# Feeding a short causal convolution: lagged rows copied between partitions instead of loaded back from memory

## The chip, the cores and the metric

One core of one Trainium2 chip. The metric is the device time of one execution in microseconds; where a kernel was run several times, the median is given. One more execution was recorded by the hardware profiler, and every duration and time of day below (us from the start of its span) is from that one.

## The reference

One step of a hybrid decoder layer for a prompt of 512 tokens, 16 meta tokens ahead of it, and 8 decode sequences of 8 tokens, all in float32. One projection of the normed tokens gives, among others, 1536 columns for the gated-DeltaNet heads (512 each for q, k and v). These go through a causal convolution of width 4 over the tokens:

```python
xpad = jnp.concatenate([conv_prev, qkv_pre], axis=1)
conv = sum(conv_w[j] * xpad[:, j:j + t] for j in range(CONV_W))
conv = jax.nn.silu(conv)
```

For the prompt `conv_prev` is zeros, for the decode sequences it is a stored state of three rows. So output row r needs the projected rows r-3, r-2, r-1 and r. q and k are then scaled to unit length per head, and the recurrence, a differential attention (paged past keys and values for the decode sequences), an output projection, and a mixture of experts follow: per token 8 heads of 16 experts out of 16384, whose two rows of 1024 are gathered.

## The kernel before

Tokens lie on partitions: four prompt tiles of 128 rows, and one tile of 80 (64 decode tokens and the 16 meta tokens), which is called the sample tile here and always comes first. The projection is cut into units, one for a section of 512 columns and a tile: 16 matmul records of PE into one of two PSUM banks. The three convolution sections come first, so there are 15 convolution tiles, numbered m = 0 to 14; m = 0, 5 and 10 are the sample tile, the other 12 are prompt tiles.

The way of one prompt tile m through the engines:

- ACT copies the unit's bank to SBUF, scaled (`unit_copy`, L1027), into `raw[:, m % 2]`, and issues the store of these 128 rows to a buffer `pre_conv` in DRAM (L1031).
- POOL waits for the stores of tiles m and m-1 and for the SiLU of tile m-2, whose buffer it reuses, and issues one load of 128 x 4 x 512 (`conv_inputs`, L935): partition r gets the rows r-3 to r, so every row of `pre_conv` is read four times. For a sample tile there are five loads (L932, L933), and ahead of them the reload of the tap weights `cw` for the section (L918), which waits for the multiply of the tile before.
- DVE multiplies the 2048 columns by the tap weights (L1444), adds them in pairs (L1446, L1447); ACT takes the SiLU (L1128) and sums squares per head (L1138); DVE adds eps (L1454), POOL takes the power -1/2 (L886), DVE scales (L1459, L1461); SP stores the tile to DRAM (L696).

In the same stretch PE works through the decode sequences' attention over the past, in four passes p = 0 to 3 (`past`: scores L2074, folding L2090, values L2102), each with DVE sums (L1638, L1639) ahead of an exponential on ACT (L1252), three small DVE steps (L1646 to L1648) and PSUM copies on ACT (L1257, L1258). The gate columns (L1829) and the first steps of the recurrence (L1901 after L1503) lie between.

The order of the instructions on every engine is fixed when the kernel is built: each helper is a generator that yields a due time and then emits its instructions, and each engine's list is made by running the generator with the smallest due time next. `conv_at(m)` is the due time of the multiply of tile m; the units' ends give it.

The stages of a run: up to some 508 us projection, convolution, past attention, the recurrence of the first tiles and the choice of experts for the first prompt tile; from there to the end POOL gathers expert rows (8 KB each for 128 tokens, L977), DVE multiplies them with the tokens (L1797) and PE adds them up (L2228), with the attention and recurrence of the later tiles in between.

Of the kernel before, what the change touches and what calls it, by code (L numbers as in the profile page):

```python
# [27 lines left out]
HW = NH * HD  # L28
# [55 lines left out]
KEPT = (6, 2)  # L84
DMA_RING = 2048


# [163 lines left out]
def hybrid_step(nc: bass.Bass, i, o, stay_table, early_table, past_table):  # L251

    ctx = ExitStack()
    with ctx:
# [234 lines left out]
        def pre_rows(t):  # L489

            if t < PT:
                r = PRE_PROMPT + META + 128 * t
                return [(0, 128, pre[r:r + 128, :])]
            return [(0, NSAMP, samp_rows[:, CONV_W - 1:, :]), (MROW, META, pre[PRE_PROMPT:PRE_PROMPT + META, :])]

        def raw_count(n):

            return sum(2 if m % NT == 0 and m < 3 * NT else 1 for m in range(n % 2, n + 1, 2))

        def conv_loads(m):  # L500

            return sum((1 if k % NT else 1 + CONV_W) for k in range(m + 1) if conv_buffer[k] == conv_buffer[m])

# [3 lines left out]

        def taps(first, rows, ch):

            return bass.AP(tensor=pre.tensor, offset=pre.offset + first * CONV + ch.start, ap=[[CONV, rows], [CONV, CONV_W], [1, HW]])  # L510

# [145 lines left out]
        with nc.Block() as block:  # L657
# [198 lines left out]
            def _(pool):  # L856
# [52 lines left out]
                def conv_inputs():  # L909
                    for m in range(3 * NT):  # L910
                        sec, n = divmod(m, NT)
                        t = ORDER[n]
                        ch = slice(sec * HW, (sec + 1) * HW)
                        yield conv_at(m) - 9
                        if n == 0:
                            if m:
                                pool.wait_ge(s_conv, 3 * (m - 1) + 1)
                            pool.dma_start(cw, i["conv_w"][0:1, :, ch].broadcast_to([128, CONV_W, HW])).then_inc(s_cw, 16)  # L918
                        yield conv_at(m) - 8
                        if conv_before(m):  # L920
                            pool.wait_ge(s_cs, conv_before(m))
                        else:
                            pool.wait_ge(s_ss, (1, 3)[m])
                        pool.wait_ge(s_raw[m % 2], 16 * raw_count(m))
                        if n:
                            pool.wait_ge(s_raw[(m - 1) % 2], 16 * raw_count(m - 1))
                        else:
                            pool.wait_ge(s_vecs, 112)
                        b = conv_buffer[m]
                        if t == PT:  # L930
                            for j in range(CONV_W):
                                pool.dma_start(cv[b][0:NSAMP, j, :], samp_rows[:, j:j + DS, ch]).then_inc(s_cv[b], 16)  # L932
                            pool.dma_start(cv[b][MROW:LAST, :, :], taps(0, META, ch)).then_inc(s_cv[b], 16)  # L933
                        else:
                            pool.dma_start(cv[b][:, :, :], taps(META + 128 * t, 128, ch)).then_inc(s_cv[b], 16)  # L935

# [43 lines left out]
            def _(act):  # L980
# [29 lines left out]
                def unit_copy(n):  # L1010
# [9 lines left out]
                    if g < 4:  # L1020
                        c = n - C0
                        if c >= 2:
                            act.wait_ge(s_raw[c % 2], 16 * raw_count(c - 2))
                        else:
                            act.wait_ge(s_ss8, c + 1)
# [92 lines left out]
                def conv_silu(m):  # L1118
# [3 lines left out]
                    yield conv_at(m) + 4.5  # L1122
                    act.wait_ge(s_conv, 3 * (m + 1))
                    if m == 1:
# [245 lines left out]
            def _(dve):  # L1370
# [66 lines left out]
                def conv(m):  # L1437
# [5 lines left out]
                    dve.wait_ge(s_cw, 16 * (sec + 1))  # L1443
                    count.done(nc.vector.tensor_tensor(x, x, cw[0:rows], ALU.mult), s_conv)  # L1444
                    yield conv_at(m) + 2.5
# [834 lines left out]
```

## Time and profile before

| | us |
|---|---|
| median of three runs | 2042.04 (2041.55 to 2044.48) |
| the profiled execution's own time | 2041.71 |
| its span | 2039.9 |
| PE busy | 1684.6 (83%) |
| DVE busy | 1350.9 (66%) |
| ACT busy | 795.9 (39%) |
| POOL busy | 770.7 (38%) |

How to read it: the span runs from the first to the last recorded event of the core. A busy share is an average over all stages, and each stage has its own limit; so the stages have to be looked at by themselves. Instructions of an engine run in program order, and idle time of an engine stands ahead of the instruction that waited, with what released it. Idle time matters only where it is handed on to the engine that paces the stage.

### The profile page before, as it was taken

How to read it: one execution, taken by the hardware profiler on the slowest of the kernel's cores; microseconds unless marked ns; L12 is line 12 of the kernel's file. 1: busy time of each engine (PE TensorE's matmuls, PEld its weight loads, DVE VectorE, ACT ScalarE, POOL GpSimd, SP SyncE). 2: the span in 40 equal slices, each digit the busy share in tenths (PEclk: the TensorE clock that was granted, in tenths of full speed). 3: DMA queues.
4: the chain of work that ended last, by engine and by line, in shares of the span. 5: the costliest groups of instructions: out<-in, count | busy, mean ns of one | idle time of the engine just before them, and what ended most of it. 6: DMA issues, size and time to landing. Idle time of an engine off the chain costs nothing.

```text
span 2039.9 us, 20195 instructions
## 1 busy us (share of the span) xinstructions
PE 1684.6 (83%) x6163; PEld 849.3 (42%) x6163; DVE 1350.9 (66%) x3035; ACT 795.9 (39%) x2359; POOL 770.7 (38%) x670
## 2 busy tenths in 40 slices
PE   7898899988998878889787888977897657866877
PEld 2334364547453344445334444533463223532211
DVE  1344514345898666887766788775698977679544
ACT  1334312222546433563543346362344433333432
POOL 2211100111444433435454353633444555554442
PEclk9998899999999988999999899998999788987999
DMA  9999623138999999999999999999999999999997
GB/s 345 369 370 369 215 79 114 47 119 330 395 423 413 428 427 428 426 420 410 427 415 429 426 426 403 420 425 394 425 427 427 427 427 427 427 427 427 427 428 314
DMA packets 137301, 759.68 MB, mean 372 GB/s; under 512 B 15295, under 2 KB 24399, under 8 KB 60760
## 3 DMA queue, kind: packets, MB, share of 16 engines
q0 software_dynamic: 88448, 622.22, 73.5%
q1 hardware_dynamic: 44112, 124.93, 16.4%
q10 hardware_dynamic: 4632, 11.23, 1.4%
q8 instruction: 49, 0.80, 0.1%
q14 instruction: 60, 0.49, 0.1%
HBM read 742.35 MB, written 16.26 MB: 372 GB/s over the span
## 4 chain that ended last, share of the span: by engine, by line
PE 34%; DMA 34%; DVE 17%; ACT 7%; issue 5%; POOL 3%; SPq 0%; ACTq 0%; DVEq 0%; POOLq 0%
DMA sb_uv<-in_peer_uv,sb_eidx 29%; PE bank L2228 14%; DVE sb_uv L1797 7%; PE bank L1818 7%; PE bank L2195 3%; DVE sb_hres L1770 2%; POOL sb_uv L977 2%; DMA sb_hres<-pre_conv 2%; ACT sb_diag L1367 1%; PE bank L2137 1%; DMA sb_w<-in_w_sections 1%; DMA sb_zone<-in_w_route 1%; PE bank L1932 1%; ACT sb_ew L1360 1%; PE bank L1944 1%
## 5 line engine op out<-in xcount | busy, mean ns | idle before, releaser
L2228 PE MATMUL bank<-sb_uv,sb_diag 128*128 128x512 f32 (+1 forms) x1812 | 926.3, 647 | 274.8 <-ACT sb_diag L1367 265.0
L977 POOL DMA_INDIRECT sb_uv<-in_peer_uv,sb_eidx x576 | 689.3, 1197 | 845.7 <-PE bank L2228 647.7
L1797 DVE CUSTOM_DVE_ANT_0 sb_uv<-sb_uv,sb_xn 128x1024 f32<-128x1024 f32 x576 | 699.6, 1220 | 295.5 <-DMA sb_uv<-in_peer_uv,sb_eidx 292.9
L2228 PEld LDWEIGHTS bank<-sb_uv,sb_diag 128*128 128x128 f32 (+1 forms) x1812 | 325.5, 195 | 756.2 <-ACT sb_diag L1367 441.8
L1356 ACT ACTIVATE sb_gel<-sb_h 128x1 f32<-128x1 f32 x576 | 116.2, 202 | 769.4 <-DVE sb_h L1797 767.0
L1818 PE MATMUL bank<-sb_w,sb_xnT 128*128 128x512 f32 (+1 forms) x560 | 267.3, 619 | 16.8 <-DVE sb_xnT L1385 8.3
L1367 ACT ACTIVATE sb_diag<-sb_stay,sb_ew 128x128 f32<-128x128 f32 (+1 forms) x453 | 178.4, 394 | 45.3 <-PE bank L2228 3.4
L1360 ACT ACTIVATE sb_ew<-sb_gel,sb_gate 128x1 f32<-128x1 f32 x576 | 169.7, 295 | 20.1 <-ACT sb_gel L1356 0.4
L1770 DVE SCALAR_TENSOR_TENSOR sb_hres<-sb_uv,sb_ew,sb_hres 128x1024 f32<-128x1024 f32 x123 | 157.5, 1281 | 4.1 <-ACT sb_ew L1360 4.1
L1818 PEld LDWEIGHTS bank<-sb_w,sb_xnT 128*128 128x128 f32 (+1 forms) x560 | 98.3, 187 | 139.7 <-issue 118.3
L2195 PEld LDWEIGHTS bank<-sb_rT,sb_zone 128*128 128x128 f32 x1024 | 124.1, 195 | 20.9 <-issue 20.1
L2195 PE MATMUL bank<-sb_rT,sb_zone 128*128 128x128 f32 x1024 | 125.6, 279 | 2.5 <-issue 1.8
L901 POOL TENSOR_TENSOR sb_rstd<-sb_ms,sb_minus_half 128x8 f32<-128x8 f32 (+1 forms) x10 | 16.4, 1642 | 113.2 <-DVE sb_ms L1472 113.2
L1797 DVE DVE_READ_ACCUMULATOR2_ANT sb_h<- 128x1 f32 x576 | 46.9, 81 | 0.0
L1356 ACT ACT_TABLE_LOAD x33 | 42.3, 1283 | 0.6
L1444 DVE TENSOR_TENSOR sb_xin<-sb_xin,sb_taps 128x2048 f32<-128x2048 f32 (+1 forms) x8 | 18.3, 2288 | 33.9 <-DMA sb_xin<-pre_conv 33.9
L1701 DVE FIND_INDEX8 sb_tix<-sb_top,sb_score 128x8 uint32<-128x128 f32 x144 | 38.4, 283 | 0.0
L1444 DVE TENSOR_TENSOR sb_hres<-sb_hres,sb_taps 128x2048 f32<-128x2048 f32 (+1 forms) x7 | 16.0, 2292 | 30.2 <-DMA sb_hres<-pre_conv 30.2
L1697 DVE MAX8 sb_top<-sb_score 128x8 f32<-128x128 f32 x144 | 31.4, 278 | 7.0 <-ACT sb_score L1328 6.9
L2137 PE MATMUL bank<-sb_mix_kept,sb_rT 128*128 128x512 f32 x64 | 31.3, 626 | 4.4 <-ACT sb_rT L1283 3.6
L1536 DVE TENSOR_TENSOR sb_X<-sb_X,bank 128x256 f32<-128x256 f32 (+1 forms) x36 | 14.7, 407 | 30.4 <-PE bank L1944 28.8
L2195 PEld LDWEIGHTS bank<-sb_rT,sb_held 128*128 128x128 f32 x256 | 31.9, 197 | 6.8 <-issue 6.8
(352 smaller groups left out, 1610.9 us busy)
## 6 DMA issues: line engine op xcount, KB each, us to landing
sb_zone<-in_w_route SPq DMA_DIRECT2D x14, 2304.0 KB, 12.2
sb_w<-in_w_sections SPq DMA_DIRECT2D x40, 512.0 KB, 8.9
sb_uv<-in_peer_uv,sb_eidx POOLq DMA_INDIRECT x576, 14.0
sb_sS<-in_cache_kT SPq DMA_DIRECT2D x32, 256.0 KB, 8.4
sb_zone<-in_cache_kT SPq DMA_DIRECT2D x32, 256.0 KB, 7.3
sb_held<-in_cache_v SPq DMA_DIRECT2D x32, 256.0 KB, 9.2
sb_zone<-in_cache_v SPq DMA_DIRECT2D x32, 256.0 KB, 9.5
sb_hres<-pre_conv POOLq DMA_DIRECT2D x6, 1024.0 KB, 8.9
```

The source lines that it names most:

```text
L977: nc.gpsimd.indirect_dma_start(uv[:, m % RING, :], None, i["peer_uv"], bass.IndirectOffsetOnAxis(ap=eidx[:, t % 2, n:n + 1], axis=0)).then ...
L1356: nc.scalar.activation(G["gel"][:, at], G["h"][:, at], ACT.Gelu).then_inc(s_dg, 1)
L1360: nc.scalar.activation(G["ew"][:, at], G["gel"][:, at], ACT.Copy, scale=gate[:, t % 2, n:n + 1]).then_inc(s_dg, 1)
L1367: nc.scalar.activation(G["diag"][:, d % DIAGS, 0:cols], eye, ACT.Copy, scale=G["ew"][:, at]).then_inc(s_dg, 1)
L1444: count.done(nc.vector.tensor_tensor(x, x, cw[0:rows], ALU.mult), s_conv)
L1701: n_used = count.inc(nc.vector.max_index(tix[:, q, k:k + 8], top[:, q, k:k + 8], sets[q]), s_cut if k and q == quads[-1] else s_tk)
L1770: nc.vector.scalar_tensor_tensor(hres[:, t % 2, :], uv[:, m % RING, D:2 * D], G["ew"][:, m % 8:m % 8 + 1], hres[:, t % 2, :], ALU.mult, AL ...
L1797: nc.vector.tensor_tensor_reduce(out=uv[:, m % RING, 0:D], in0=uv[:, m % RING, 0:D], in1=xn2[:, t % 2, :], scale=1.0, scalar=0.0, op0=ALU. ...
L1818: ins = nc.tensor.matmul(bank[b][0:rows, :], lhsT=xT(t)[:, kk, :], rhs=F["w"][:, piece % PIECES, kk % 2, :], start=kk == 0, stop=kk == KC - 1)
L2137: ins = nc.tensor.matmul(bank[6 + half][:, :], lhsT=R["rT"][:, k, :], rhs=mixer_row(n, half, k), start=k == 0, stop=k == KC - 1)
L2195: ins = nc.tensor.matmul(bank[6 + j % 2][:, 128 * s:128 * s + 128], lhsT=weights_part(n, g + 2)[:, k, 128 * s:128 * s + 128], rhs=R["rT"][ ...
L2228: ins = nc.tensor.matmul(bank[half][0:rows, :], lhsT=G["diag"][:, d % DIAGS, 0:rows], rhs=uv[:, m % RING, D + 512 * half:D + 512 * half + ...
```

## The change

For the 12 prompt tiles the taps no longer come from DRAM. Three copies within SBUF, issued by POOL, take rows j to j+124 of `raw` to partitions 3 to 127 of tap j (j = 0, 1, 2). Tap 3, which has no lag, is not copied: DVE multiplies it straight out of `raw`. Only what crosses a tile's edge goes through DRAM: ACT stores the first and the last three rows of a tile (two stores of 3 rows instead of one of 128), and POOL loads 3 rows x 3 taps for partitions 0 to 2. So a prompt tile has four POOL-issued transfers instead of one, and the multiply is two instructions. Counts of the semaphores follow. The reuse of `raw` by ACT now also waits for the multiply of the tile that used it before. The sample tiles are unchanged.

```diff
+EDGE = CONV_W - 1
...
             if t < PT:
                 r = PRE_PROMPT + META + 128 * t
-                return [(0, 128, pre[r:r + 128, :])]
+                return [(first, EDGE, pre[r + first:r + first + EDGE, :]) for first in (0, 128 - EDGE)]
...
         def raw_count(n):
-            return sum(2 if m % NT == 0 and m < 3 * NT else 1 for m in range(n % 2, n + 1, 2))
+            return sum(2 if m < 3 * NT else 1 for m in range(n % 2, n + 1, 2))
+        def conv_steps(m):
+            return sum(4 if k % NT else 3 for k in range(m))
         def conv_loads(m):
-            return sum((1 if k % NT else 1 + CONV_W) for k in range(m + 1) if conv_buffer[k] == conv_buffer[m])
+            return sum((CONV_W if k % NT else 1 + CONV_W) for k in range(m + 1) if conv_buffer[k] == conv_buffer[m])
...
-        def taps(first, rows, ch):
-            return bass.AP(tensor=pre.tensor, offset=pre.offset + first * CONV + ch.start, ap=[[CONV, rows], [CONV, CONV_W], [1, HW]])
+        def taps(first, rows, ch, many=CONV_W):
+            return bass.AP(tensor=pre.tensor, offset=pre.offset + first * CONV + ch.start, ap=[[CONV, rows], [CONV, many], [1, HW]])
...
                         yield conv_at(m) - 9
                         if n == 0:
                             if m:
-                                pool.wait_ge(s_conv, 3 * (m - 1) + 1)
+                                pool.wait_ge(s_conv, conv_steps(m - 1) + 2)
                             pool.dma_start(cw, i["conv_w"][0:1, :, ch].broadcast_to([128, CONV_W, HW])).then_inc(s_cw, 16)
-                        yield conv_at(m) - 8
+                        yield conv_at(m) - (12.2 if n else 8)
                         if conv_before(m):
                             pool.wait_ge(s_cs, conv_before(m))
                         else:
                             pool.wait_ge(s_ss, (1, 3)[m])
+                        if n:
+                            bank_of, copies = entry_bank("unit", C0 + m)
+                            pool.wait_ge(s_bank[bank_of], copies + 1)
+                            for j in range(EDGE):
+                                pool.dma_start(cv[conv_buffer[m]][EDGE:128, j, :], F["raw"][j:j + 128 - EDGE, m % 2, :]).then_inc(s_cv[conv_buffer[m]], 16)
+                            yield conv_at(m) - 8.6
                         pool.wait_ge(s_raw[m % 2], 16 * raw_count(m))
...
-                            pool.dma_start(cv[b][:, :, :], taps(META + 128 * t, 128, ch)).then_inc(s_cv[b], 16)
+                            pool.dma_start(cv[b][0:EDGE, 0:EDGE, :], taps(META + 128 * t, EDGE, ch, EDGE)).then_inc(s_cv[b], 16)
...
                             act.wait_ge(s_raw[c % 2], 16 * raw_count(c - 2))
+                            if (c - 2) % NT and c - 2 < 3 * NT:
+                                act.wait_ge(s_conv, conv_steps(c - 2) + 2)
...
-                    act.wait_ge(s_conv, 3 * (m + 1))
+                    act.wait_ge(s_conv, conv_steps(m + 1))
...
-                    count.done(nc.vector.tensor_tensor(x, x, cw[0:rows], ALU.mult), s_conv)
+                    if n:
+                        count.inc(nc.vector.tensor_tensor(x[:, 0:EDGE], x[:, 0:EDGE], cw[0:rows, 0:EDGE], ALU.mult), s_conv)
+                        count.done(nc.vector.tensor_tensor(x[:, EDGE], F["raw"][0:rows, m % 2, :], cw[0:rows, EDGE], ALU.mult), s_conv)
+                    else:
+                        count.done(nc.vector.tensor_tensor(x, x, cw[0:rows], ALU.mult), s_conv)
```

## Rows read from the trace of the kernel before

**Rows 1.** Busy time by stage: length; PE, PEld, DVE, ACT, POOL; clock, DMA share, GB/s.

```profile
72.00:262.00 190.00, 172.76 (x770) 76.51 (x767) 92.26 (x128) 72.46 (x195) 33.02 (x39) 0.94 0.89 321
262.00:508.00 246.00, 228.00 (x1114) 143.62 (x1112) 94.97 (x262) 57.50 (x146) 28.77 (x24) 0.99 0.38 137
508.00:2039.00 1531.00, 1233.34 (x4140) 612.12 (x4140) 1148.03 (x2620) 651.63 (x1986) 692.20 (x578) 0.93 1.00 418
```

**Rows 2.** Timeline of PE, 112 to 240 us: start, length, instruction [idle before, releaser].

```profile
112.73 1.03 PE L1829 MATMUL bank<-sb_xnT,sb_wba 128*8 128x512 f32 x4 [1.85 <-DVE sb_held L1639]
...
118.64 1.89 PE L2090 MATMUL bank<-sb_held 128*128 128x64 f32 x16
...
161.26 3.67 PE L2090 MATMUL bank<-sb_held 128*128 128x64 f32 x16 [5.38 <-DVE sb_held L1648]
...
209.52 1.07 PE L2102 MATMUL bank<-sb_held 128*32 128x512 f32 x2 [5.87 <-ACT sb_held L1258]
...
239.34 0.77 PE L1901 MATMUL bank<-sb_stay,sb_kb 80*128 80x80 f32 x4 [3.35 <-DVE sb_kb L1503]
```

**Rows 3.** The chain that ended last, around 170 us: start, length, what.

```profile
165.34 3.63 PE bank L1818 x4
...
174.37 1.87 PE bank L1818 x4
```

**Rows 4.** Timeline of DVE: multiplies of m = 3, 4, 5, 6, 9, 10 and 13.

```profile
107.07 2.29 DVE L1444 TENSOR_TENSOR sb_hres<-sb_hres,sb_taps 128x2048 f32<-128x2048 f32 x1 [4.78 <-DMA sb_hres<-pre_conv]
...
110.66 0.69 DVE L1447 TENSOR_TENSOR sb_hres<-sb_hres 128x512 f32<-128x512 f32 x1
...
123.03 2.29 DVE L1444 TENSOR_TENSOR sb_xin<-sb_xin,sb_taps 128x2048 f32<-128x2048 f32 x1 [4.70 <-DMA sb_xin<-pre_conv]
...
141.88 2.29 DVE L1444 TENSOR_TENSOR sb_hres<-sb_hres,sb_taps 80x2048 f32<-80x2048 f32 x1 [10.56 <-DMA sb_hres<-pre_conv]
...
150.13 2.28 DVE L1444 TENSOR_TENSOR sb_xin<-sb_xin,sb_taps 128x2048 f32<-128x2048 f32 x1
...
188.32 2.29 DVE L1444 TENSOR_TENSOR sb_hres<-sb_hres,sb_taps 128x2048 f32<-128x2048 f32 x1 [2.50 <-DMA sb_hres<-pre_conv]
...
203.96 2.29 DVE L1444 TENSOR_TENSOR sb_xin<-sb_xin,sb_taps 80x2048 f32<-80x2048 f32 x1 [5.16 <-DMA sb_xin<-pre_conv]
...
236.18 2.29 DVE L1444 TENSOR_TENSOR sb_hres<-sb_hres,sb_taps 128x2048 f32<-128x2048 f32 x1 [5.75 <-DMA sb_hres<-pre_conv]
```

**Rows 5.** Timeline of POOL: loads of m = 3, 4, 5 and 13, weights' reload.

```profile
95.41 0.78 POOL L935 DMA_DIRECT2D sb_hres<-pre_conv  x1 [7.29 <-issue]
...
112.08 0.79 POOL L935 DMA_DIRECT2D sb_xin<-pre_conv  x1 [10.51 <-ACT sb_cs L1128]
...
125.78 0.79 POOL L918 DMA_DIRECT2D sb_taps<-in_conv_w  x1 [10.58 <-DVE sb_xin L1444]
126.56 2.29 POOL L932 DMA_DIRECT2D sb_hres<-pre_conv  x4
...
228.94 0.80 POOL L935 DMA_DIRECT2D sb_hres<-pre_conv  x1
```

**Rows 6.** Timeline of ACT's DMA issues: stores of m = 3 and 5.

```profile
87.40 0.33 ACTq L1031 DMA_DIRECT2D pre_conv<-sb_raw  x1
...
113.92 1.11 ACTq L1031 DMA_DIRECT2D pre_conv<-sb_raw  x2
```

**Rows 7.** DMA issues of the whole span: KB each, median us from issue to landing.

```profile
sb_hres<-pre_conv POOLq DMA_DIRECT2D x6, 1024.0 KB, 8.9
...
sb_stay<-stay_tables ACTq DMA_DIRECT2D x1, 816.0 KB, 10.9
...
sb_hres<-pre_conv POOLq DMA_DIRECT2D x5, 128.0 KB, 10.7
...
sb_held<-sb_held ACTq DMA_DIRECT2D x1, 32.0 KB, 6.9
...
pre_conv<-sb_qst POOLq DMA_DIRECT2D x3, 6.0 KB, 3.2
```

## The prediction

> **What bounds the kernel now.** I read the kernel by stages first [rows 1]. The last and longest stage, 508 to 2039 us, has its DMA engines busy all the time (share 1.00, 418 GB/s): it streams expert rows, its length is given by bytes, and the change does not touch it. The stage before it, 262 to 508, has PE busy 228 of 246 us and DMA at 0.38. All the work of the change lies in the first stage, and the table's row for 72 to 262 says what to look for there: PE busy 172.8 of 190 us, at a mean clock of 0.94, beside DMA at 0.89 and DVE, ACT and POOL each under half. So PE paces that stretch, with holes, and a microsecond of hole filled there reaches the end of the run if the two later stages simply start sooner.
>
> Next the order of PE's instructions, for the holes [rows 2]: 1.85 us ahead of L1829, 5.38 ahead of L2090, 5.87 ahead of L2102, 3.35 ahead of L1901, 16.5 us in all. None is a wait for DMA; all are for DVE or ACT. Behind the second hole PE also runs at the lower of its two clock levels (1.2 instead of 2.4 GHz): the 16 matmuls of L2090 take 3.67 us where they took 1.89 at 118.64 [rows 2], and four of L1818 take 3.63 where they take 1.87 a little later [rows 3]: 3.5 us on top of the hole.
>
> Then what made DVE and ACT late. DVE runs in program order, and its long idle times stand ahead of the tap multiply L1444, waiting for loaded taps [rows 4]: 10.56 us at 141.88, 5.16 at 203.96, 5.75 at 236.18. POOL's rows [rows 5] give the other half: it issues the load of tile m=3 at 95.41 after idling 7.29 us, although ACT issued that tile's store at 87.40 [rows 6]. From store to multiply (107.07) is **19.7 us: about 8 for the store, 11.7 for the load** [rows 4 to 6].
>
> **The change, part by part.**
>
> *Bytes.* A prompt tile stored 256 KB and loaded 1024; it will move 3 x 250 KB on chip, store 12 KB and load 18: 500 KB less, 6.1 MB over 12 tiles. At 321 GB/s over a share of 0.89, so 361 at full share [rows 1], that is 17 us of DMA time. No hole of PE waits for DMA directly, so I count none of it; it can only shorten landings.
>
> *ACT.* One store becomes two. Two issues took 1.11 us from 113.92, one takes 0.33 [rows 6]: 0.78 us more per prompt tile. ACT has room for 9 us [rows 1], but the copy of m=8 stands right ahead of the exponential that the second hole waits for: 0.78 is charged there. The new wait of the copy of tile m+2 for the multiply of m costs nothing: ACT's own order has the SiLU of m, which waits for that multiply and the sums behind it, ahead of that copy. If that cover went, PE's next unit would wait for its bank.
>
> *POOL.* One issue of 0.79 us becomes four; the nearest rows, four of 64 rows in 2.29 and the 0.79 itself [rows 5], give 0.57 each, 2.3 in all: 1.5 more per tile, 18 in total, beside 33 busy of 190 [rows 1]. The order hardly moves: the copies are written as due at 12.2 before the multiply, but the stream has first to pass its step at 9 before it, so they stand where the load stood, behind the same power step of tile m-2 and ahead of that of m-1. Only tile 1's copies pass tile 0's power step. Queued behind the edge load's wait for the store is again the power of m-1, as before.
>
> *DVE.* 2048 columns in 2.29 us become 1536 and 512. Between the 512-column 0.69 and 2.29 [rows 4] a line gives 1.76 for 1536: 2.45 in all, 0.16 more per tile.
>
> *The edge's way.* Store 6 KB, wait, load 18 KB. From below, both land as the 6 KB store did early in the run, 3.2 us each [rows 7]: 7.7 us with 1.3 of issues. From above, they are as slow as now: 8 for the store, 10.7 for a 128 KB load [rows 7] and 0.6: 19.3, no gain. I take 6 us each, 13.3 in all, because the smallest transfer made under load, 32 KB, landed in 6.9 [rows 7].
>
> *The copies.* No copy of this size from SBUF to SBUF is in the trace. The 32 KB one took 6.9 us, the 1 MB load 8.9 [rows 7]. I take 9 behind 1.7 us of issues, 10.7 after ACT's copy; less than 13.3, so the edge sets the time. Ends: 6.9, and several times 9 (below). They need no store to have landed.
>
> The Trainium skill (DMA: Bandwidth & Descriptors, section "Why a DMA increments its semaphore by 16 and not by 1") speaks against the copies: a transfer is spread over the largest number of engines up to 16 that divides the slowest dimension, which is 5 for 125 rows, though it also tells of GpSimd copies on trn2 that kept 16. No row here shows a transfer of such a row count; by the first reading it is the second rival, by the other the sum stands.
>
> So a tap multiply can start some 6 us sooner after its projection, where nothing else is late. **At each hole:**
>
> A. L1829 waits for a DVE sum that stands behind m=3's multiply (107.07 [rows 4]). 6 us sooner, that hole is gone: 1.85.
>
> B. m=4's load was issued only at 112.08 [rows 5], because its store queued behind two table loads (L998, L999) on ACT's queue, the larger of which took 10.9 us [rows 7]. The edge stores queue there too, but the tables are issued behind the SiLU of m=2, which comes 4 to 6 us sooner. So the edge can be there about 114, and DVE was free at 118.33 (123.03 less 4.70) [rows 4], before A. I take m=4's multiply 6 us sooner; bounds 4.7 and 7.1. At that multiply hangs a chain that the change leaves alone: reload of the tap weights (125.78 [rows 5]), five loads of the sample tile m=5, its multiply at 141.88, m=6's directly behind it at 150.13, the exponential, L2090. All of it moves 6 us. PE resumes at 161.26 - 6 + 0.78 = 156.0: 5.2 gained, A within it. What is left of the hole is 2.8 us beside an otherwise earlier PE; I take it that the clock then stays up: 3.5. Together 8.7.
>
> C. The same chain at the third section: m=9's multiply waited 2.50 us for its load [rows 4]; that goes, then DVE's order is late next. Weights, five loads, m=10's multiply (203.96) and L2102 come 2.4 us sooner against the rest.
>
> D. m=13's load went out at 228.94, behind a power step of the decode part that stays, when DMA is light. Copies to 230.7, edge load to 231.2, landing 3.2 to 4 later, about 235 against 236.18: 1.2.
>
> Sum: 8.7 + 2.4 + 1.2 = **12.3 us**. The profiled execution took 2041.71 us, 0.33 under the median of the runs shown, which is nothing here: 2041.7 - 12.3 = 2029.4. I say **2029**.
>
> **The rivals.**
>
> *Hidden by the sample tiles.* The waits at 141.88 and 203.96 are for the loads of m=5 and m=10, which the change doesn't touch. If m=4 and m=9 gain nothing, since the edge store is held up behind the tables or small transfers under load are as slow as big ones, A and D remain: 2041.7 - 3.1 = 2038.6. For it: the upper bound of the edge. Against it: m=4 and m=9 do wait for loads on DVE.
>
> *Copies on few engines, no gain.* A 1 MB load puts 64 KB on each of 16 engines and lands in 8.9 us, 5.7 more than the 3.2 of a tiny one. If all three copies share five engines, each carries 150 KB: 3.2 + 13.4 = 16.6, and with 2.4 of copy and issues 19 us, what it is now. Then only the bytes are saved: about 2040. (If each takes another five, 50 KB each, the forecast stands.) This is what the Trainium skill's rule would do at its worst here.
>
> *Slower: one engine per copy.* Then it carries 250 KB, 22.3 + 3.2 = 25.5 us, so 28 after the projection's copy instead of 19.7. The multiply of m=4 (copy ready about 101) would come near 129 instead of 123, of m=9 near 200 instead of 188, of m=13 some 8 us late: 26 us, 2068. It decides from a landing of about 16 us on. Against it: nothing in the copies but their odd row count and their shift between partitions.
>
> *All holes close.* Lighter DMA brings the sample tiles sooner as well: 16.5 + 3.5 = 20 us, 2022, or a little below with clock losses that I left out.
>
> *The change doesn't do what it says,* for instance the copies wait for something that I took as done: 2042.
>
> **How the numbers follow.** 0.2%, 4 us, is about what a measurement of this kernel can tell from no change. Forecast 0.58, with its own range of 2021 to 2036; hidden 0.15, a third of it over 4 us faster; no gain 0.06; slower 0.10; all holes 0.08; nothing 0.03. Faster: 0.58 + 0.05 + 0.08 = 0.71; same: 0.10 + 0.06 + 0.03 = 0.19; slower 0.10. The range 2019 to 2042 takes in the forecast, the two cases without much gain, no effect and most of the closed holes: more than 8 in 10 on its face; I leave it, since the copy's landing has no row.
>
> **What the profile would show.** Right: the three copies land within 12 us of their issue; L1444 of m=4 starts by 118 and of m=5 by 137; the hole ahead of L2090 is under 3 us and its 16 matmuls take about 1.9; m=1 to 4 and 6 to 9 start some 6 us sooner after their projection; the last stage keeps its length. Wrong: copies that land after 16 us or more, POOL idle ahead of the power steps, or an equal gain at 262 that is gone at 508.

## The result, and the profile of the changed kernel

The changed kernel takes **2049.76 us** (median of 8 runs, 2045.77 to 2057.36) against 2042.25 for the kernel before beside it: ratio 1.0038, 95% interval 1.0022 to 1.0054. It is slower by 7.5 us where 13 less were forecast. Its profiled execution took 2051.02 us, with a span of 2049.2.

Busy time by stage after, columns as in [rows 1]:

```profile
72.00:262.00 190.00, 164.70 (x753) 72.15 (x752) 91.41 (x137) 70.50 (x189) 50.11 (x71) 0.93 0.90 289
262.00:508.00 246.00, 230.90 (x1126) 144.53 (x1124) 92.26 (x250) 57.31 (x147) 28.82 (x24) 0.99 0.37 133
508.00:2049.00 1541.00, 1239.69 (x4140) 614.76 (x4140) 1151.15 (x2632) 652.48 (x1988) 699.42 (x578) 0.93 1.00 416
```

In the first row PE did 8.1 us less work than before (172.76 in [rows 1]). Its last two figures are the ones to stop at: the DMA engines are as busy, 0.90 against 0.89, but move 289 GB/s instead of 321. A tenth fewer bytes take the same time.

PE's timeline after, the instructions with holes (they answer to [rows 2]; PE's line numbers are 17 higher):

```profile
109.84 3.70 PE L1835 MATMUL bank<-sb_w,sb_xnT 128*80 128x512 f32 x4 [9.61 <-DMA sb_w<-in_w_sections]
...
168.36 0.62 PE L2119 MATMUL bank<-sb_held 128*32 128x512 f32 x2 [0.82 <-DMA sb_zone<-in_cache_v]
...
185.60 9.30 PE L1835 MATMUL bank<-sb_w,sb_xnT 128*80 128x512 f32 x16 [8.89 <-DMA sb_w<-in_w_sections]
...
214.15 0.62 PE L2119 MATMUL bank<-sb_held 128*32 128x512 f32 x2 [0.71 <-ACT sb_held L1271]
...
243.16 0.77 PE L1918 MATMUL bank<-sb_stay,sb_kb 80*128 80x80 f32 x4 [5.25 <-DVE sb_kb L1520]
```

[rows 2] leave out a fifth hole of the kernel before, a short one that waits for ACT:

```profile
148.74 7.13 PE L1818 MATMUL bank<-sb_w,sb_xnT 128*128 128x512 f32 x16 [0.78 <-ACT sb_raw L1027]
```

The old holes of 1.85, 5.38 and 0.78 us are gone and 5.87 became 0.71: 13.2 us. Two new ones, 9.61 and 8.89, both wait for **the weights of the next section**; with 0.82, and 1.9 more ahead of L1918, that is 21.2. The balance is 8 us, the work that PE lacks above.

The first of these weights on SP's queue, timeline before:

```profile
91.69 1.57 SPq L687 DMA_DIRECT2D sb_w<-in_w_sections  x2
```

And in the changed kernel's chain that ended last (start, length, what):

```profile
91.73 18.07 DMA sb_w<-in_w_sections
109.84 3.70 PE bank L1835 x4
```

The issue stands at the same time in both kernels; the landing takes 18.07 us, and PE waits for its end. The second hole is another matter in part. Its weights on SP's queue, before and after:

```profile
166.93 1.86 SPq L687 DMA_DIRECT2D sb_w<-in_w_sections  x4
```

```profile
172.36 3.88 SPq L692 DMA_DIRECT2D sb_w<-in_w_sections  x4
```

They go out 5.4 us later and land in 13.7 instead of 12.1 us (medians of the four), so most of that hole comes from the late issue.

The traffic around the first moment, 78 to 112 us: packets, MB and their time as a share of 16 engines (q1 is SP's queue, q0 POOL's), then issues with KB and median us to landing. Before:

```profile
DMA packets 5614, 13.39 MB, mean 394 GB/s; under 512 B 596, under 2 KB 596, under 8 KB 5611
...
q1 hardware_dynamic: 4241, 8.47, 65.7%
q0 software_dynamic: 650, 2.47, 19.6%
...
sb_w<-in_w_sections SPq DMA_DIRECT2D x4, 512.0 KB, 11.5
```

After:

```profile
DMA packets 4872, 11.36 MB, mean 334 GB/s; under 512 B 705, under 2 KB 705, under 8 KB 4869
...
q1 hardware_dynamic: 3729, 7.32, 66.1%
q0 software_dynamic: 816, 2.34, 24.0%
...
sb_w<-in_w_sections SPq DMA_DIRECT2D x3, 512.0 KB, 18.1
...
sb_xin<-sb_raw POOLq DMA_DIRECT2D x6, 250.0 KB, 8.2
```

A share times 34 us over its MB is the **price of a megabyte** in time of all 16 engines. It is no cost in isolation: with ACT's queue the shares add up to over 100% (103 before, 104 after), so packets of different queues overlap, and a packet's time can hold some waiting. POOL's queue went from 2.70 us (0.196 x 34 / 2.47) to 3.49, and SP's queue, which does what it did, from 2.64 to 3.07. Over single packets of this stretch, the median of POOL's 4096-byte ones rose from 168 to 227 ns, the mean of SP's 2048-byte ones from 87 to 100.

The same rows for the whole front, up to the first gather of the experts, columns as above (q10 is ACT's queue). Before, 0 to 485.6:

```profile
q1 hardware_dynamic: 38592, 80.37, 46.7%
q0 software_dynamic: 5504, 18.20, 11.7%
q10 hardware_dynamic: 4632, 11.23, 6.0%
```

After, 0 to 488.6:

```profile
q1 hardware_dynamic: 38592, 80.37, 48.5%
q0 software_dynamic: 5696, 15.06, 11.3%
q10 hardware_dynamic: 3048, 8.23, 4.5%
```

Share times stretch gives 226.8 + 56.8 + 29.1 = 312.7 us before and 237.0 + 55.2 + 22.0 = 314.2 after. The stores saved 7 us; POOL's queue saved 1.6, with 17% fewer bytes; SP's unchanged traffic became 10 us dearer. **The change moves 6.1 MB less and uses no less DMA time.**

### The profile page after: what moved, and what is told of

Same layout as the page of the kernel before. It is cut to its first block, busy times and chain, and to the rows that moved or that the text cites. A ratio compares the mean times of both kernels' runs of the same rounds, so it can differ in the third digit from the quotient of the medians.

```text
span 2049.2 us, 20269 instructions
## 1 busy us (share of the span) xinstructions
PE 1687.2 (82%) x6163; PEld 849.3 (41%) x6163; DVE 1351.8 (66%) x3047; ACT 796.1 (39%) x2359; POOL 796.7 (39%) x706
## 4 chain that ended last, share of the span: by engine, by line
PE 37%; DMA 31%; DVE 14%; ACT 7%; issue 4%; SPq 4%; POOL 2%; ACTq 0%; DVEq 0%; POOLq 0%
DMA sb_uv<-in_peer_uv,sb_eidx 27%; PE bank L2245 15%; PE bank L1835 7%; DVE sb_uv L1814 6%; PE bank L2212 3%; DMA sb_w<-in_w_sections 2%; PE bank L2154 2%; POOL sb_uv L988 2%; SPq L837 1%; DVE sb_hres L1787 1%; ACT sb_diag L1380 1%; SPq L824 1%; ACT sb_ew L1373 1%; DMA sb_zone<-in_w_route 1%; SPq L819 1%
## 5 line engine op out<-in xcount | busy, mean ns | idle before, releaser
L988 POOL DMA_INDIRECT sb_uv<-in_peer_uv,sb_eidx x576 | 697.3, 1211 | 843.0 <-PE bank L2245 651.9
L2212 PE MATMUL bank<-sb_rT,sb_held 128*128 128x128 f32 x256 | 31.2, 275 | 0.0
L1949 PEld LDWEIGHTS bank<-sb_X,sb_MT 128*128 128x128 f32 (+1 forms) x184 | 23.0, 186 | 16.6 <-issue 16.6
## 6 DMA issues: line engine op xcount, KB each, us to landing
sb_zone<-in_w_route SPq DMA_DIRECT2D x14, 2304.0 KB, 12.1
sb_zone<-in_cache_v SPq DMA_DIRECT2D x32, 256.0 KB, 10.3
```

The costliest lines, as they stand in the source:

```text
L988: nc.gpsimd.indirect_dma_start(uv[:, m % RING, :], None, i["peer_uv"], bass.IndirectOffsetOnAxis(ap=eidx[:, t % 2, n:n + 1], axis=0)).then ...
L2212: ins = nc.tensor.matmul(bank[6 + j % 2][:, 128 * s:128 * s + 128], lhsT=weights_part(n, g + 2)[:, k, 128 * s:128 * s + 128], rhs=R["rT"][ ...
```

## The experiments

They ask in turn whether the copies are the cause, what makes them dear, whether their moment counts, and whether a better version follows. "Price" is that of POOL's queue in 78 to 112 us, worked out as above (before 2.70, after 3.49 us per MB). Ratios are to the kernel before, whose median was 2040.7 to 2042.2 beside these runs. The cuts of the code are shortened: `b` stands for `conv_buffer[m]`, and semaphore increments and their counts are left out. "The whole result" marks runs that leave no lag out. The expectations speak of two holes of 3.70 and 9.30 us, 13.0 in all; these are the lengths of the matmuls behind the holes. The holes are 9.61 and 8.89, 18.5 in all.

**No copies.**

```diff
-for j in range(EDGE):
-    pool.dma_start(cv[b][EDGE:128, j, :], F["raw"][j:j + 128 - EDGE, m % 2, :])
-tensor_tensor(x[:, 0:EDGE], x[:, 0:EDGE], cw[0:rows, 0:EDGE], ALU.mult)
+tensor_tensor(x[:, 0:EDGE], F["raw"][0:rows, m % 2, :].unsqueeze(1).broadcast_to([rows, EDGE, HW]), cw[0:rows, 0:EDGE], ALU.mult)
```

> The changed kernel without its 36 copies: the multiply reads the projection's buffer for all four taps (the lags of rows 3 to 127 are left out; every instruction of DVE, every store and every edge load stays). All theories of the front's transfers (copies are dear, or uneven, or shifted): the first weights of sections m = 5 and m = 10 land as early as before or earlier, the two holes ahead of L1835 (3.70 and 9.30 us) shrink to under 2 us in all, the 2.3 us holes ahead of the transposes stay away, and the mark at the first gather of the experts comes at 475 to 481 us (changed kernel 488.6, kernel before 485.6); the whole is some 8 to 12 us below the changed kernel's, so 2030 to 2036 us against the kernel before's 2042. Rival, the holes come from the new order on POOL's and ACT's queues or from the edge loads and not from copies: the holes stay near 13 us and the mark at 487 to 489. If the part of the loss behind the first gather (6 us of 9) belongs to the change and not to the run, it shows here too.

Measured: **2016.49 us**, 0.9876 (0.9856 to 0.9896): 33 us under the changed kernel, three times what was expected; the first gather comes at 459.3 instead of 488.6. The weights' matmuls as a group, 72 to 262 us (count, busy, mean ns, idle before), in the changed kernel:

```profile
L1835 PE MATMUL bank<-sb_w,sb_xnT 128*128 128x512 f32 (+1 forms) x233 | 111.7, 626 | 18.5 <-DMA sb_w<-in_w_sections 18.5
```

Without copies:

```profile
L1833 PE MATMUL bank<-sb_w,sb_xnT 128*128 128x512 f32 (+1 forms) x278 | 126.9, 600 | 0.0
```

The loss goes with the copies: ACT's split store, its wait, the edge loads and the two multiplies are all still there. DMA queues without copies up to the first gather, 0 to 459.3:

```profile
q1 hardware_dynamic: 38594, 80.40, 50.6%
q0 software_dynamic: 2816, 5.84, 4.9%
q10 hardware_dynamic: 3048, 8.23, 4.7%
```

The front's DMA time is 276.5 us, 37.7 less than in the changed kernel, and 33 of it reach the end, though no hole in [rows 2] names a DMA. That is no fixed rate: from before to after 1.5 us more came with 7.5 at the end, and the early copies of 128 rows below have 298.8 us, 13.9 less than before, for 4.9 at the end. SP's own traffic takes 232.4 us here, still 5.6 more than before: of the 10 us by which it became dearer, 4.6 go with the copies, and what the other 5.6 are no run shows.

**Source in memory; no shift.** Two runs, each with one edit to the copy:

```diff
-pool.dma_start(cv[b][EDGE:128, j, :], F["raw"][j:j + 128 - EDGE, m % 2, :])
+pool.dma_start(cv[b][EDGE:128, j, :], i["x_prompt"][0, j:j + 128 - EDGE, 0:HW])
```

> The changed kernel with only the source of the 36 copies changed: the same 125 rows of 2 KB to the same places at the same moments, after the same wait, but out of a prompt input in memory instead of the projection's buffer (so the lagged taps of rows 3 to 127 hold tokens and not the projection). Theory 1, a packet between partitions is slow in itself (median 229 ns against 169 for the 1 MB load of before) and slows the other queues: POOL's 4096-byte packets go back to 165 to 180 ns, the front's rate comes back from 334 to over 370 GB/s in the stretch 78 to 112, the holes ahead of L1835 fall from 13.0 to under 4 us, first gather at 476 to 482 us, whole 2031 to 2038. Theory 2, it is the volume and the moment of 750 KB per tile: packets and holes as in the changed kernel, first gather 487 to 490, whole 2046 to 2052.

```diff
-pool.dma_start(cv[b][EDGE:128, j, :], F["raw"][j:j + 128 - EDGE, m % 2, :])
+pool.dma_start(cv[b][EDGE:128, j, :], F["raw"][EDGE:128, m % 2, :])
```

> The changed kernel with copies of 125 rows from partition p to partition p instead of p-1, p-2 and p-3 (the lags of rows 3 to 127 are left out). Theory, the shift of partitions makes the copies dear (a packet's read and write lie at different places): packets fall from 229 ns towards 170, holes ahead of L1835 from 13.0 to under 5 us, first gather at 477 to 483 us. Theory, any copy from SBUF to SBUF is dear: nothing changes, packets 220 to 240 ns, holes 11 to 15 us, first gather 487 to 490, whole 2047 to 2052 us.

Measured: 2049.04 us, 1.0031 (1.0018 to 1.0044), price 3.39; and 2048.06, 1.0029 (1.0010 to 1.0047), price 3.53. POOL's queue with the source in memory, 78 to 112 us:

```profile
q0 software_dynamic: 816, 2.34, 23.3%
```

Neither the on-chip source nor the shift makes the copies dear. Theory 1 falls.

**Three taps from memory.** The whole result: full store, no copies, one load of 3 taps in place of 4, sent where the kernel before sends its load; last tap from the projection's buffer.

```diff
-return [(first, EDGE, pre[r + first:r + first + EDGE, :]) for first in (0, 128 - EDGE)]
+return [(0, 128, pre[r:r + 128, :])]
...
-yield conv_at(m) - (12.2 if n else 8)
+yield conv_at(m) - 8
...
-for j in range(EDGE):
-    pool.dma_start(cv[b][EDGE:128, j, :], F["raw"][j:j + 128 - EDGE, m % 2, :])
...
-pool.dma_start(cv[b][0:EDGE, 0:EDGE, :], taps(META + 128 * t, EDGE, ch, EDGE))
+pool.dma_start(cv[b][:, 0:EDGE, :], taps(META + 128 * t, 128, ch, EDGE))
```

> A version that computes the whole result: the full row block of 256 KB is stored as in the kernel before, the three lagged taps come from memory in one load of 768 KB, and only the tap without lag is read from the projection's buffer; no copy between partitions. Against the kernel before it moves 256 KB (a quarter of the load) less per prompt tile and waits for the same store. If copies are what costs: the landing of the loads shrinks from 8.9 to about 7.5 us, so L1458 starts about 1.5 us earlier than the multiply before, weights land as before (no hole over 1 us ahead of L1835), first gather 480 to 485, whole 2034 to 2041, a gain of 1 to 8 us against the kernel before. If the loss lies in the two multiplies, the waits on s_conv or ACT's added wait, which this version keeps: whole 2044 to 2050, like the changed kernel.

Measured: **2034.92 us**, 0.9969 (0.9956 to 0.9983): faster than both kernels. Its traffic in 78 to 112 us:

```profile
DMA packets 5955, 13.59 MB, mean 400 GB/s; under 512 B 661, under 2 KB 661, under 8 KB 5952
...
q1 hardware_dynamic: 4778, 9.48, 73.4%
...
q0 software_dynamic: 454, 1.66, 12.7%
```

Price 2.60. And the queues up to its first gather, 0 to 472.5:

```profile
q1 hardware_dynamic: 38594, 80.40, 48.2%
q0 software_dynamic: 4736, 15.06, 9.9%
q10 hardware_dynamic: 4632, 11.23, 6.2%
```

The front's DMA time is 303.8 us: 8.9 less than before, for 6.5 at the end. One hole for weights stays, 3.21 us at 172.87, where none over 1 us was expected.

**One copy of three taps.**

```diff
-for j in range(EDGE):
-    pool.dma_start(cv[b][EDGE:128, j, :], F["raw"][j:j + 128 - EDGE, m % 2, :])
+pool.dma_start(cv[b][EDGE:128, 0:EDGE, :], F["raw"][EDGE:128, m % 2, :].unsqueeze(1).broadcast_to([128 - EDGE, EDGE, HW]))
```

> The changed kernel with the three copies of a tile made one: one transfer writes all three taps of 125 partitions, 6 KB side by side in each, out of the same rows of the projection's buffer (from partition p to p, so the lags of rows 3 to 127 are left out, as in the run without the shift). Same bytes, same wait, same moment; 62.5 packets of 2 partitions per tap become 187.5 packets that lie in one partition. Theory A, the form (2 KB to each partition, a packet across two of them) makes a packet cost 229 ns instead of 170 and slows its neighbours: packets go to 165 to 185 ns, the two holes ahead of L1835 go from 13.0 to under 5 us, whole 2022 to 2034 us. Theory B, it is 125 rows instead of 128, or SBUF to SBUF, or the early moment: nothing changes, whole 2045 to 2052 us.

Measured: 2090.35 us, 1.0239 (1.0218 to 1.0259), price 4.44, the worst of all: the single copy lands in 10.3 to 12.3 us, and the trace has 751 packets of 8 bytes on POOL's queue in 78 to 112, where the changed kernel has 35. Where these come from is open; neither theory had them. PE does not lose its time ahead of the weights here (0.93 us) but behind DVE, whose multiplies wait for taps; the edge loads land in 15.5 and 22.6 us. In PE's timeline:

```profile
134.47 1.88 PE L1845 MATMUL bank<-sb_xnT,sb_wba 128*8 128x512 f32 x4 [18.18 <-DVE sb_held L1655]
```

**Memory in three loads.** As "three taps from memory", with:

```diff
-pool.dma_start(cv[b][:, 0:EDGE, :], taps(META + 128 * t, 128, ch, EDGE))
+for j in range(EDGE):
+    pool.dma_start(cv[b][:, j, :], taps(META + 128 * t + j, 128, ch, 1)[:, 0, :])
```

> The whole result, as in the version with three taps in one load from memory (2034.9 us), but that load of 768 KB made into three of 128 rows of 2 KB, one per tap. Theory A (form): packets go from 172 to about 225 ns, weights' landing from 11.7 to over 14 us, a hole over 5 us ahead of the weights' matmuls, whole 2043 to 2055 us: slower than the one load by 8 to 20. Theory B (125 rows, source or moment): as the one load, 2033 to 2039, only two more issues of 0.55 us on POOL per tile.

Measured: 2039.75 us, 0.9989 (0.9973 to 1.0005), price 2.65, packets 162 ns. Theory A (form) falls: 2 KB to a partition is cheap here. The 5 us against one load go with PE's holes behind DVE and ACT and not with waits for weights: 4.31, 3.57 and 4.98 us where one load has 2.44, 0.97 and 1.96.

**112 rows; copies later.**

```diff
-pool.dma_start(cv[b][EDGE:128, j, :], F["raw"][j:j + 128 - EDGE, m % 2, :])
+pool.dma_start(cv[b][16:128, j, :], F["raw"][16:128, m % 2, :])
```

> The changed kernel with three copies of 112 rows (16 times 7) from partition p to p in place of 125 rows (rows 3 to 15 of the lagged taps keep what the buffer held, the other lags are left out). 10% fewer bytes. Theory, 125 rows share out unevenly over the 16 engines: packets fall to 170 to 185 ns, weights land within 13 us, holes ahead of L1835 from 12 to 16 us (run without the shift: 12.1) to under 5, whole 2025 to 2036. Theory A (form) or early moment: packets stay over 215 ns, holes 9 to 13 us, whole 2041 to 2050 (a few us less than without the shift at 125 rows, for the bytes).

```diff
-for j in range(EDGE):
-    pool.dma_start(cv[b][EDGE:128, j, :], F["raw"][j:j + 128 - EDGE, m % 2, :])
 pool.wait_ge(s_raw[m % 2], 16 * raw_count(m))
 pool.wait_ge(s_raw[(m - 1) % 2], 16 * raw_count(m - 1))
+for j in range(EDGE):
+    pool.dma_start(cv[b][EDGE:128, j, :], F["raw"][j:j + 128 - EDGE, m % 2, :])
```

> The whole result; the changed kernel with the three copies issued behind the two waits for the stores, together with the edge load, so some 4 to 7 us later and no longer right behind the projection. Theory, the moment: copies sent earlier than the load of before collide with the section's weights; then weights of m = 5 and m = 10 land in 11 to 14 us, holes ahead of L1835 under 6 us, whole 2034 to 2043. Theory A (form): the packets stay at 220 to 235 ns and the sum of the holes at 11 to 16 us, some of them now ahead of L1658-type waits for the copies; whole 2047 to 2056.

Measured: 112 rows 2043.65 us, 1.0010 (0.9999 to 1.0020), price 3.61: no cheaper per byte although 16 divides 112. Later copies 2042.62, 1.0006 (0.9995 to 1.0018), price 3.71: as dear, yet 7 us better at the end. Its two weights' holes became one, in PE's timeline:

```profile
180.09 9.21 PE L1835 MATMUL bank<-sb_w,sb_xnT 128*80 128x512 f32 x16 [8.04 <-DMA sb_w<-in_w_sections]
```

That hole is 8.04 us where under 6 was expected, and 4.01 us for cached keys (`in_cache_kT`, at 147.28) come on top. So for dear copies the moment is worth some 7 us beside the price: sent right behind the projection they collide with the weights' landing.

**128 rows.** The cheap loads had 128 rows, the dear ones 125 or 112. Three runs; the edge load is out in each:

```diff
-pool.dma_start(cv[b][EDGE:128, j, :], F["raw"][j:j + 128 - EDGE, m % 2, :])
+pool.dma_start(cv[b][:, j, :], F["raw"][:, m % 2, :])
...
-pool.dma_start(cv[b][0:EDGE, 0:EDGE, :], taps(META + 128 * t, EDGE, ch, EDGE))
```

> The changed kernel with three copies of all 128 rows, partition p to p, out of the projection's buffer at the same early moment, and without the edge load of 18 KB that they cover (the lags of every row are left out). 2.4% more bytes than the 125 rows without the shift (packets 231 ns, 2048.1 us). Theory C, it is the rows of a transfer: with 128 rows, 8 for each of 16 engines, an engine keeps to a fixed block of partitions, with 125 or 112 the blocks lie across it; packets fall from 229 to 160 to 185 ns, the packets of the weights' queue from a mean of 98 to under 90, the holes ahead of L1835 from 12 to under 3 us, whole 2020 to 2034. Rival, copies that are sent so early are dear whatever their rows: packets 215 to 240, whole 2044 to 2052.

```diff
-pool.dma_start(cv[b][EDGE:128, j, :], F["raw"][j:j + 128 - EDGE, m % 2, :])
+pool.dma_start(cv[b][:, j, :], i["x_prompt"][0, 0:128, 0:HW])
```

> The run with the source in memory (125 rows of a prompt input, packets 227 ns, 2049.0 us) with 128 rows in place of 125, at the same early moment, without the edge load (lagged taps hold tokens). Theory C: packets 160 to 185 ns, whole 2020 to 2034 and within 5 us of the 128 rows from the projection's buffer, so that the source costs nothing. Rival, moment: 215 to 240 ns, 2044 to 2052.

```diff
-pool.dma_start(cv[b][EDGE:128, j, :], F["raw"][j:j + 128 - EDGE, m % 2, :])
+for r in (0, 64):
+    pool.dma_start(cv[b][r:r + 64, j, :], F["raw"][r:r + 64, m % 2, :])
```

> As the copies of 128 rows, but each made as two of 64 rows (partitions 0 to 63 and 64 to 127): 6 transfers per tile, 4 rows for each of 16 engines, nothing left over, but an engine's rows now lie elsewhere than in the 128-row transfers. Theory C (fixed block of partitions for each engine): packets stay dear, 200 to 240 ns, whole 2040 to 2056. Rival, a number of rows that leaves a remainder over 16 engines or an odd packet is what costs: packets 160 to 185 ns, whole 2022 to 2038, with 1.7 us more of issues on POOL per tile.

Measured: 128 rows from the projection's buffer **2035.74 us**, 0.9976 (0.9964 to 0.9988), price 2.52; early from memory 2035.83, 0.9966 (0.9950 to 0.9983), price 2.74; the same rows as two halves 2053.28, 1.0066 (1.0047 to 1.0084), price 3.80. The traffic with 128 rows, 78 to 112 us:

```profile
q1 hardware_dynamic: 4044, 8.13, 66.9%
q0 software_dynamic: 720, 2.36, 17.5%
...
sb_w<-in_w_sections SPq DMA_DIRECT2D x4, 512.0 KB, 12.4
```

The early load of 128 rows from memory:

```profile
q0 software_dynamic: 720, 2.36, 19.0%
```

And twice 64:

```profile
q0 software_dynamic: 831, 2.29, 25.6%
...
sb_w<-in_w_sections SPq DMA_DIRECT2D x3, 512.0 KB, 18.3
```

Three more rows per copy and no edge load: 12 us less than the 125 unshifted rows, and the weights land in 12.4 us (before 11.5). The edge load is not what divides them: the two halves have none either and are dear. Theory C had the side right, but both times are some 2 us above its range and one hole of 7.68 stays where under 3 was expected, in PE's timeline with 128 rows:

```profile
106.71 3.70 PE L1833 MATMUL bank<-sb_w,sb_xnT 128*80 128x512 f32 x4 [7.68 <-DMA sb_w<-in_w_sections]
```

**The kernel before again.**

> The kernel before, unchanged, for a second profile. If the 6 us that the changed kernel's profile loses behind the first gather (1560.6 us from the first gather to the end against 1554.3) are scatter of that stage, this profile takes 1556 to 1563 there and first gathers at 480 to 487; if the change slows that stage, it takes 1553 to 1556. Whole 2036 to 2047 us.

Measured: 2043.37 us. The first gathers of POOL (start) in its timeline and in the changed kernel's:

```profile
482.62 1.09 POOL L977 DMA_INDIRECT sb_uv<-in_peer_uv,sb_eidx  x1 [18.33 <-DVE sb_eidx L1754]
```

```profile
488.60 1.09 POOL L988 DMA_INDIRECT sb_uv<-in_peer_uv,sb_eidx  x1 [18.34 <-DVE sb_eidx L1771]
```

From there to the end it took 1559.0 us, against 1554.3 in the first profile and 1560.6 in the changed kernel's. So the 6 us that the changed kernel seemed to lose in the last stage are that stage's scatter (all 17 profiles lie between 1552.9 and 1563.5); against this second profile the front alone is 6.0 us later.

**Which property of 128.** Three more runs: 128 rows sent later, 120 rows from partition 8 (the whole result), 125 rows from partition 0.

```diff
-for j in range(EDGE):
-    pool.dma_start(cv[b][EDGE:128, j, :], F["raw"][j:j + 128 - EDGE, m % 2, :])
...
 pool.wait_ge(s_raw[(m - 1) % 2], 16 * raw_count(m - 1))
+for j in range(EDGE):
+    pool.dma_start(cv[b][:, j, :], F["raw"][:, m % 2, :])
...
-pool.dma_start(cv[b][0:EDGE, 0:EDGE, :], taps(META + 128 * t, EDGE, ch, EDGE))
```

> Both at once: copies of all 128 rows from p to p without the edge load (lags left out), issued behind the waits for the stores as in the run with later copies. Corners so far: 125 rows early 2048 to 2050, 125 later 2042.6, 128 early 2035.7. If rows and moment add up: 2028 to 2031 us, no hole over 2 us ahead of the weights' matmuls. If the later moment only helped because it eased the collision of dear packets: 2033 to 2038, like 128 early.

```diff
-return [(first, EDGE, pre[r + first:r + first + EDGE, :]) for first in (0, 128 - EDGE)]
+return [(first, many, pre[r + first:r + first + many, :]) for first, many in ((0, 8), (128 - EDGE, EDGE))]
...
-pool.dma_start(cv[b][EDGE:128, j, :], F["raw"][j:j + 128 - EDGE, m % 2, :])
+pool.dma_start(cv[b][8:128, j, :], F["raw"][j + 8 - EDGE:j + 128 - EDGE, m % 2, :])
...
-pool.dma_start(cv[b][0:EDGE, 0:EDGE, :], taps(META + 128 * t, EDGE, ch, EDGE))
+pool.dma_start(cv[b][0:8, 0:EDGE, :], taps(META + 128 * t, 8, ch, EDGE))
```

> The whole result: the changed kernel with the copies cut to partitions 8 to 127 (120 rows, the lag in the source), and 8 rows instead of 3 at the tile's head through memory. If a transfer is dear when an engine's run of rows straddles blocks of 8 partitions, and 120 rows fall to 15 engines in runs of 8 that begin on a block: packets 160 to 185 ns, whole 2033 to 2038, like 128 early rows. If it is dear whenever an engine writes to a block that is another engine's in the 128-row transfers (or if 120 rows are dealt out 7.5 to each of 16): 205 to 250 ns, whole 2045 to 2052.

```diff
-pool.dma_start(cv[b][EDGE:128, j, :], F["raw"][j:j + 128 - EDGE, m % 2, :])
+pool.dma_start(cv[b][0:128 - EDGE, j, :], F["raw"][0:128 - EDGE, m % 2, :])
...
-pool.dma_start(cv[b][0:EDGE, 0:EDGE, :], taps(META + 128 * t, EDGE, ch, EDGE))
+pool.dma_start(cv[b][128 - EDGE:128, 0:EDGE, :], taps(META + 128 * t, EDGE, ch, EDGE))
```

> The changed kernel with its 125 rows written to partitions 0 to 124, p to p, and the 3 edge rows written to partitions 125 to 127 (lags left out, the same bytes and transfers). If the start decides, 16 runs of 8 rows (the last of 5) that begin where those of a 128-row transfer begin: packets 160 to 185 ns, whole 2033 to 2039. If the count of 125 decides (run lengths that aren't 8): 215 to 240 ns, whole 2045 to 2052.

Measured: 128 later 2033.77 us, 0.9964 (0.9949 to 0.9979), price 2.65; 120 rows 2053.63, 1.0057 (1.0039 to 1.0074), price 3.52; 125 from partition 0 2050.54, 1.0036 (1.0023 to 1.0049), price 3.60. Later is worth some 2 us once the copies are cheap, which is within the scatter of the two: mostly it eased the collision of dear packets. Neither the start nor blocks of 8 decide; both of my guesses at what makes rows cheap fell, and the dear side came out in each. Among the runs with copies or loads of lagged taps there is none between 2.74 and 3.39 us per MB: **all with 128 rows lie below, all with 125, 120, 112 or 64 above, whatever the source, shift, start and moment.** All of them were issued by POOL; no other queue and no other row counts were tried.

Why 128 is shown by no run, since the trace does not say which engine or port a packet used. The Trainium skill ("DMA: Bandwidth & Descriptors", section "The descriptor swizzle") states that in a transfer of 128 partitions each of the 16 engines writes one port of the SBUF, and refers to another section for other shapes. That section of the Trainium skill, "Why a DMA increments its semaphore by 16 and not by 1", gives each engine a sixteenth of the partitions, rounded up, in some GpSimd copies on trn2. A guess from the two: if the dear copies are of that kind and an engine's partitions lie side by side, two engines can be at one port at a time. That 128 rows alone were cheap and twice 64 dear fits the guess, but no run tests it.

## Why the prediction was wrong

**The step that failed** is the one on bytes: "No hole of PE waits for DMA directly, so I count none of it; it can only shorten landings." A rate of 361 GB/s was applied to bytes that the new transfers don't move at that rate, and what they cost was left out as if beside the path. In the runs the front's DMA time did not fall (312.7 to 314.2 us), the first weights' landing grew to 18.07 us, and PE waited 18.5 us for weights. A sign was on view: a DMA share of 0.89 [rows 1] leaves little slack (over 72 to 110 us alone it is 1.04), and the multiplies that made DVE late waited for loads themselves [rows 4]. In the second profile of the kernel before, PE did wait for DMA, 1.11 us at 143.33 and 1.77 for weights at 177.60.

The chain that the prediction drew behind m=4's multiply was sound; it shows where the transfer is cheap. With three taps in one load of 128 rows, which sends no copies and gains 6.5 us, m=4's multiply starts at 117.78 and m=5's at 136.19 (forecast 118 and 137), the hole ahead of the folding is 2.44 us (under 3) and its 16 matmuls take 2.00 (1.9).

**Right in size:** the instructions. Three copies issue in 1.65 us and the edge load in 0.60, 2.25 for the 2.3 forecast; POOL's busy time grew by 17.1 us (50.11 less 33.02) for 18; DVE's two multiplies take 1.76 and 0.69, as worked out; a copy lands in 6.9 to 8.2 us (forecast 9) and the edge load in 6.5 (6). The edge store was mis-sized at m=4: issued at 97.08, it held POOL's edge load back to 111.05, some 14 us where 6 were taken.

```profile
111.05 0.60 POOL L946 DMA_DIRECT2D sb_xin<-pre_conv  x1 [11.62 <-DMA pre_conv<-sb_raw]
```

**A held in part, B, C and D did not.** m=3's multiply did move, in DVE's timeline after:

```profile
98.54 1.76 DVE L1458 TENSOR_TENSOR sb_hres<-sb_hres,sb_taps 128x1536 f32<-128x1536 f32 x1
...
116.42 0.69 DVE L1655 TENSOR_TENSOR sb_held<-bank,sb_bias_past 128x512 f32<-128x512 f32 x1 [12.94 <-PE bank L2096]
...
124.05 1.75 DVE L1458 TENSOR_TENSOR sb_xin<-sb_xin,sb_taps 128x1536 f32<-128x1536 f32 x1
...
142.37 2.29 DVE L1461 TENSOR_TENSOR sb_hres<-sb_hres,sb_taps 80x2048 f32<-80x2048 f32 x1 [6.70 <-DMA sb_hres<-pre_conv]
...
239.93 1.76 DVE L1458 TENSOR_TENSOR sb_hres<-sb_hres,sb_taps 128x1536 f32<-128x1536 f32 x1 [7.34 <-DMA sb_hres<-pre_conv]
```

It comes 8.5 us sooner than in [rows 4] and waits for nothing. But m=4's was to start by 118 and started at 124.05, behind a DVE step that waited 12.94 us for PE, which waited for weights; m=5's at 142.37 instead of 137. The hole ahead of L2107 closed not because DVE came sooner (its last step starts at 161.75, where it started at 160.95 in the kernel before) but because PE came later. At C, m=9's multiply lost its wait and came 4 us sooner, at 184.35, but m=10's came 4.6 later, at 208.58, and PE reached L2119 at 214.15 instead of 209.52. D failed as well: m=13's multiply starts 3.75 us later than before.

**The rivals.** "Hidden by the sample tiles" had its condition met at m=4, where the edge store was held up, but it did not set the time: m=4's multiply waited for no load. "Slower: one engine per copy" had the side right and the mechanism wrong: the copies landed in 8 us, far below its 16. "Copies on few engines" had the right subject, the row count of a transfer, but looked for it in the copies' own landing; it came out in the weights'.

## What to carry to other kernels

In a stage whose DMA share is near 0.9, price a transfer by its engines' time and not by its bytes, and do not leave it out because no hole names a DMA: here 37.7 us of it were worth 33 in one run, 13.9 worth 5 in another. Give a transfer to SBUF 128 rows if that can be had: from POOL's queue other row counts cost 3.4 to 3.8 us per MB for 2.5 to 2.7, and SP's packets were slower beside them. For the lagged rows that meant a 128-row load from memory, 15 us better than the copies (2034.92 against 2049.76), with only the unshifted operand read where it lies.

## What the runs showed that was not expected

- A copy between partitions costs no more than a load from memory when both have 128 rows: 2.52 against 2.74 us per MB.
- Dear packets spread: SP's 80.4 MB of the front took 237.0 us beside 125-row copies and 229.6 beside 128-row ones (226.8 in the kernel before, 232.4 without copies).
- One transfer of 125 x 6 KB with a repeated source cost more than three of 125 x 2 KB: 2090.35 against 2048.06 us, for a reason that is open.
- The last stage scatters by 10 us between profiles, so a difference of a few us is read up to the first gather, or over many runs.
